# RMS norms moved into the stages that use them, and an earlier gate evacuation in the RWKV rounds, in a two-layer decoder trunk

## What is computed

```
for l in range(DEPTH):
    xn = rmsnorm(h, norm_mix_w[l])
    h = h + hybrid_mixer(xn, ...)      # RG-LRU, gated DeltaNet, RWKV-7, three sigmoid merge gates
    xn = rmsnorm(h, norm_ffn_w[l])
    h = h + peer_ffn(xn, ...)          # product-key top-k, gated experts
return rmsnorm(h, final_norm_w)

def rmsnorm(x, w):
    return x * lax.rsqrt(jnp.mean(x * x, axis=-1) + 1e-6) * w
```

## Time and profile before

| | us |
|---|---|
| median of 3 runs | 3383.24 |
| lowest, highest | 3376.41, 3383.72 |
| the profiled execution | 3370.82 |
| its span, first instruction to last | 3368.9 |
| PE busy in the span | 3245.6 |
| DVE busy | 2270.9 |
| ACT busy | 1673.8 |
| POOL busy | 161.2 |

### The profile page before, as it was taken

One profiled execution on the slowest core, in us unless ns is written; L12 is line 12 of the kernel. 1 busy time (PEld: TensorE's weight loads), 2 busy tenths in 40 slices (PEclk: granted clock), 3 DMA queues, 4 the chain that ended last, 5 costly groups with the idle time before them and its releaser, 6 DMA issues. The chain is left out here.

```text
span 3368.9 us, 73580 instructions
## 1 busy us (share of the span) xinstructions
PE 3245.6 (96%) x24714; PEld 2813.4 (84%) x24714; DVE 2270.9 (67%) x5009; ACT 1673.8 (50%) x3549; POOL 161.2 (5%) x169
## 2 busy tenths in 40 slices
PE   8999999999999999999999999999999999999998
PEld 7777778889998888888878777888898978888886
DVE  5666666655886677777666665666658866777776
ACT  5445454433296555555544443544423955555554
POOL 0101101100000000000001101011000000000000
PEclk9999999999999999999999999999999999999999
DMA  3322323223323555555432323232242245555553
GB/s 130 96 74 80 109 78 104 88 82 144 107 81 128 190 187 187 187 189 192 155 127 66 99 68 104 82 107 75 94 169 83 75 149 188 187 187 191 191 190 126
DMA packets 122237, 433.35 MB, mean 129 GB/s; under 512 B 15744, under 2 KB 18048, under 8 KB 121344
## 3 DMA queue, kind: packets, MB, share of 16 engines
q1 hardware_dynamic: 122112, 431.74, 37.4%
HBM read 430.64 MB, written 1.05 MB: 128 GB/s over the span
## 5 line engine op out<-in xcount | busy, mean ns | idle before, releaser
L2265 PE MATMUL bank<-x_both,u_parts 128*128 128x512 f32 x1536 | 557.9, 397 | 1.4 <-DVE u_parts L2385 1.4
L2249 PE MATMUL bank<-v_parts,act_high 128*128 128x512 f32 x1024 | 405.6, 396 | 4.6 <-DVE v_parts L2390 3.4
L2251 PE MATMUL bank<-v_parts,act_low 128*128 128x512 f32 x1024 | 400.0, 391 | 0.0
L2261 PE MATMUL bank<-x_both,u_parts 128*128 128x256 f32 x1536 | 399.6, 281 | 0.0
L2250 PE MATMUL bank<-v_parts,act_high 128*128 128x512 f32 x1024 | 398.9, 390 | 0.0
L298 PE MATMUL bank<-x_parts,w_parts 128*128 128x256 f32 x1248 | 394.2, 316 | 1.5 <-DVE w_parts L286 1.5
L2385 DVE TENSOR_TENSOR u_parts<-u_raw,u_parts 128x512 fp32r<-128x512 f32 x384 | 265.4, 692 | 191.6 <-ACT u_parts L2320 191.5
L299 PE MATMUL bank<-x_parts,w_parts 128*128 128x256 f32 x1248 | 352.3, 282 | 0.0
L300 PE MATMUL bank<-x_parts,w_parts 128*128 128x256 f32 x1248 | 351.4, 282 | 0.0
L2390 DVE TENSOR_TENSOR v_parts<-v_raw,v_parts 128x512 fp32r<-128x512 f32 x512 | 329.7, 685 | 28.8 <-ACT v_parts L2327 25.6
L263 PE MATMUL bank<-arena,ring 128*128 128x256 f32 x1408 | 326.3, 385 | 19.8 <-ACT zg L793 9.7
(11 more groups left out here) (353 smaller groups left out, 5650.9 us busy)
## 6 DMA issues: line engine op xcount, KB each, us to landing
v_raw<-in_v SPq DMA_DIRECT2D x256, 512.0 KB, 3.5
u_raw<-in_u SPq DMA_DIRECT2D x192, 512.0 KB, 4.1
ring<-in_w_side SPq DMA_DIRECT2D x80, 512.0 KB, 3.5
ring<-in_w_gdn SPq DMA_DIRECT2D x64, 512.0 KB, 3.5
ring<-in_w_rwkv SPq DMA_DIRECT2D x48, 512.0 KB, 5.7
ring<-in_w_gdn_side SPq DMA_DIRECT2D x32, 512.0 KB, 3.5
ring<-in_u SPq DMA_DIRECT2D x32, 512.0 KB, 3.7
u_ring<-in_u SPq DMA_DIRECT2D x32, 512.0 KB, 3.5
```

What stands on the lines that cost most here:

```text
L2249: te.matmul(ps, f32r(w_hi), f32r(x_hi), start=start, stop=False, **kw)
L2251: return te.matmul(ps, f32r(w_lo), f32r(x_hi), start=False, stop=stop, **kw)
L2261: return te.matmul(banks[r % 4][:, T:2 * T], f32r(u_lo[:, cols]), f32r(xhigh[:, k]), start=False, stop=stop)
L2265: mm = te.matmul(banks[r % 4][:, :].rearrange("p (x t) -> p x t", x=2), f32r(u_hi[:, cols]), f32r(x_both[:, :, k]), start=(k == 0), stop=( ...
```

## The change

**The norms.** `rmsnorm` becomes a class `Norm` with a method for each engine. "mixnorm" is called at the head of `rwkv_phase`'s block, "ffnnorm" at the head of `peer_topk_phase`'s; "outnorm" stays a block. With that

- the barrier between a norm and its stage is gone; every consumer waits for the tiles it needs (`ready` for tile k, `all_ready`);
- DVE multiplies tiles 0 and 1, then 2 to 4; POOL tile 5, then 6 and 7; POOL also waits for ACT's last `hw`;
- ACT takes the constant's root right behind its squares, then `hw` 0 to 4, then the root of the means, then `hw` 5 to 7;
- PE runs 15 identity matmuls where it ran 22 (none in outnorm, as before);
- mixnorm's buffers lie in `zg`, so that SP issues the parameters right behind the weight tiles.

**The rounds.** `act_side(a, i, 3)` and a root of one constant column go ahead of the wait for the variance. In the last round PE gets two more identity matmuls at level 5 and six in the state steps.

```diff
+    class Norm:
+    VEC = 5
+    def vector(self, v):
...
+        for a, b in ((0, 2), (2, self.VEC)):
+            self.scaled(v, slice(a, b)).then_inc(V.sem, V.one(f"x{a}"))
+    def tensor(self, te, idle):
...
+        turn(te, banks[1], idle)
+    def scalar(self, a):
...
+        a.activation(self.root, ones[:, 0:1], ACT.Sqrt).then_inc(S.sem, S.one())
+        weighted(range(self.VEC))
+        a.wait_ge(V.sem, V.at("ms"))
+        a.activation(rs, rs, ACT.Sqrt).then_inc(S.sem, S.one("root"))
+        weighted(range(self.VEC, KT))
+    def gpsimd(self, g):
+        g.wait_ge(self.S.sem, self.S.at(f"hw{KT - 1}"))
+        g.wait_ge(self.V.sem, self.V.at("rs"))
+        for a, b in ((self.VEC, self.VEC + 1), (self.VEC + 1, KT)):
+            self.scaled(g, slice(a, b)).then_inc(self.G.sem, self.G.one(f"x{a}"))
...
@@ rwkv_phase @@
+                rwkv_first_tiles(sp, l)
                 sp.dma_start(consts64[:, :], A["consts64"]).then_inc(pload, 16)
...
-                    elif lev and y == 0:
+                    elif lev and (y == 0 or lev == 5):
...
                     if q:
+                        if not more:
+                            turn(te, b4, 1)
                         te.wait_ge(V.sem, V.at(f"S{q - 1}", i))
...
                         side(2 * q + 7)
+                        if not more:
+                            turn(te, b4, 1)
                         te.wait_ge(V.sem, V.at(f"R{q}", i))
...
+                norm.tensor(te, 15)
                 te.wait_ge(wload, 32)
...
+                act_side(a, i, 3)
+
+                a.activation(no_root, ones[:, 0:1], ACT.Sqrt).then_inc(S.sem, S.one())
                 a.wait_ge(V.sem, V.at("var", i))
                 a.activation(va4, va4, ACT.Sqrt).then_inc(S.sem, S.one("sd"))
-                act_side(a, i, 3)
...
+                norm.vector(v)
+                norm.all_ready(v)
...
@@ peer_topk_phase @@
+                query_first_loads(sp, l)
                 clear(sp, mixer_sems)
...
+                norm.tensor(te, 15)
                 te.wait_ge(query_loaded_keys, 16)
...
+                            if t == 0:
+                                norm.ready(te, k)
```

More of the change, by code:

```diff
@@ L202, in rmsnorm, with branch_buffers @@
+    def branch_buffers():
         r = Region(BRANCH)
[L203 to L206, removed]
+        return r(KT, T), r(KT, T), r(T), r(1)
+    def rmsnorm(tag, w, dst):
+        norm = Norm(tag, w, dst, branch_buffers())
         with nc.Block() as block:
[L208 to L211, removed]
@@ L213, in _ @@
             @block.vector
             def _(v):
[L215 to L221, removed]
@@ L222, in _ @@
-                scaled(v, slice(0, VEC)).then_inc(V.sem, V.one())
-                v.wait_ge(V.sem, V.now())
+                norm.vector(v)
+                norm.all_ready(v)
             @block.tensor
             def _(te):
[L227 to L231, removed]
@@ L232, in _ @@
-                mm.then_inc(E.sem, E.one("ss"))
-                if ahead:
-                    turn(te, banks[1], 22)
+                norm.tensor(te, 0)
             @block.scalar
             def _(a):
[L238 to L242, removed]
@@ L244, in _ @@
-                a.activation(root, ones[:, 0:1], ACT.Sqrt).then_inc(S.sem, S.one())
-                a.wait_ge(V.sem, V.at("ms"))
-                a.activation(rs, rs, ACT.Sqrt).then_inc(S.sem, S.one("root"))
+                norm.scalar(a)
             @block.gpsimd
             def _(g):
-                g.wait_ge(V.sem, V.at("rs"))
-                scaled(g, slice(VEC, KT)).then_inc(G.sem, G.one())
-                g.wait_ge(G.sem, G.now())
+                norm.gpsimd(g)
     def turn(te, ps, n):
@@ L563, in rwkv_phase @@
     def rwkv_phase(l):
+        norm = Norm("mixnorm", norm_w[:, 2 * l], xn, (zg[:, 0], zg[:, 1], zg[:, 2, 0], zg[:, 2, 1, 0:1]))
         NI = KT
@@ L934, in _ @@
                 te.sem_inc(W.used, W.PRIME)
+                norm.tensor(te, 15)
                 te.wait_ge(wload, 32)
                 for s in range(2):
-                    project(te, banks[2 + s][:, 0:T], 6 + s).then_inc(E0.sem, E0.one(f"lora{s}"))
+                    for k in range(KT):
+                        if s == 0:
+                            norm.ready(te, k)
+                        mm = project(te, banks[2 + s][:, 0:T], 6 + s, ks=range(k, k + 1))
+                    mm.then_inc(E0.sem, E0.one(f"lora{s}"))
                 E.prime(te)
@@ L1025, in _ @@
             def _(a):
+                norm.scalar(a)
                 for k in range(0, KT, KT // 2):
+                    if k:
+                        norm.all_ready(a)
+                    else:
+                        norm.ready(a, 0)
+                        norm.ready(a, 2)
                     a.activation(f32r(x_parts[:, 0, k:k + KT // 2]), xn[:, k:k + KT // 2], ACT.Copy).then_inc(x_high, 1)
@@ L1921, in peer_topk_phase, with _ @@
         flat = lambda x: x.rearrange("p h k -> p (h k)")
+        norm = Norm("ffnnorm", norm_w[:, 2 * l + 1], xf[:, :], branch_buffers())
         with nc.Block() as block:
+            @block.gpsimd
+            def _(g):
+                norm.gpsimd(g)
             @block.vector
```

44 lines of the change are left out of this document (39 added, 5 removed).

## The result

| | us |
|---|---|
| before, median of 20 runs | 3377.41 (3374.43 to 3383.72) |
| after, median of 20 runs | 3388.06 (3382.21 to 3396.24) |
| ratio after / before, 95% interval | 1.0030 (1.0023 to 1.0037) |
| profiled execution of after | 3388.44, span 3386.6 |

The forecast was 3379.6 and the range 3368 to 3388: the time is outside by a hair, and its sign is the wrong one. Over the 20 runs of after the time follows the mean granted clock: 3382.21 us at 0.995, 3396.24 at 0.990.

The account below looks back on a forecast made before the run. PE, busy 3245.6 of 3368.9 us, was taken to bound the kernel. Norms -13.9, looped rounds +8.5 and last rounds +1.8 summed to -3.6 us, from 3383.24 giving 3379.6 us; range 3368 to 3388.

Parts of the forecast that it names:

- first mixnorm, means to gates: First layer's mixnorm: the gates start at 26.4 us instead of 29.99, -3.6 us.
- second mixnorm, the same: Second layer's mixnorm: by the same sum 1697.55 us instead of 1699.93, -2.4 us.
- first ffnnorm, means to the first key scores: First layer's ffnnorm: first query tile done by 803.45 us instead of 806.0, -2.55 us.
- second ffnnorm: Second layer's ffnnorm: query tiles done earlier, idle stretch and lower clock gone, -4.9 us; 1.6 lost if the clock falls.
- outnorm, means to the end: Outnorm: table load leaves the path (0.48 us), less 0.1 for POOL's second instruction, -0.4 us.
- 14 looped rounds: Looped RWKV rounds' end: table loads make the root 0.97 us late, +0.61 us a round, 8.5 us lost.
- 2 last rounds: Last RWKV rounds: L923 +0.27 us, three of eight new identity matmuls +0.65, together +0.9 each, +1.8 us.
- the clock at the round's end: Rival, ahead of L923: PE's idle stretch grows to 1.4 us, TensorE falls to 1.2 GHz, 1.6 us each; 3403 us; chance 0.08.
- The costly load: Rival, round's end: a table switch holds ACT some 1.4 us more than its row, +38 us, 3418 us; chance 0.03.

Follow-up runs that it names:

- the second trace of before: The kernel before, unchanged, executed once more for another trace; 3377.12 us.
- the kernels with late roots: The kernel before with eight, or four, roots of a constant between ACT's wait for the variance and the root; 3405.6 us with eight, 3390.42 us with four.
- the one trace: Trace of the changed kernel without the constant's root, f3 still evacuated first; median 3377.4 us, ratio 0.9999 to the kernel before.

## Why the prediction was wrong, point by point

| step | forecast | measured (profiles) |
|---|---|---|
| first mixnorm, means to gates | -3.6 | -3.7 |
| second mixnorm, the same | -2.4 | -2.5 |
| first ffnnorm, means to the first key scores | -2.55 | -2.4 |
| second ffnnorm | -4.9 | -4.7 |
| outnorm, means to the end | -0.4 | -0.9 |
| 14 looped rounds | +0.61 each | +0.57 each |
| 2 last rounds | +0.9 each | +0.3 (first layer's) |
| **sum** | **-3.6** | **-5.6** |
| falls of the clock at round ends | 0 | +9.9 |
| PE's branch, and the low clock behind it | 0 | +4.3 |
| first means later, at the start of the run | 0 | +1.2 |

The lower part is 15.4 us; with the sum it gives +9.8, the medians differ by 10.7. The two agree in part by chance, for the table is made from two single traces, and the two profiled executions differ by 17.6; the 8 us between are mostly falls at the GDN stages' edges and ends (6.7 us), a kind that the second trace of before has too. The last row isn't the change's: the first means come at 14.92 and 15.03 us in the kernels with late roots as well, whose first norm is that of before (14.13 and 13.96).

- **The mechanisms stood.** Rows 1 to 5 and 7 to 10 gave each step within 0.6 us. The second layer's query tiles kept their clock, as the sum had it (timeline after, it answers rows 5):

```profile
2489.54 0.42 DVE L216 TENSOR_SCALAR arena<-bank 128x256 f32<-128x256 f32 x1 [3.21 <-PE bank L229]
...
2494.47 3.62 PE L2133 MATMUL bank<-xf,ring 128*128 x28 [0.57 <-DVE xf L209]
...
2497.93 0.39 PE L2119 MATMUL bank<-arena 128*128 128x128 f32 x2
```

From the means to the first key scores (L2119) it is 8.39 us, where it was 13.10 before.

- **The step that failed is the clock at the round's end, a term that the sum put at nothing.** It stood as a rival only. It was named with its place, its price (1.6 us; measured 1.65) and the point from which it decides (seven rounds; six fell), and given 0.08. The argument against it was that stretches of 2.2 us stood elsewhere once with a fall and once without, and that 1.4 is well under either. That compared single stretches, while the pair at the round's end (1.36 and 0.29, with 0.44 of work between) comes fourteen times, and a place that falls once in two times at 2.2 us was no proof of safety at 1.4. In its place the runs show six falls, +9.9 us, over the whole 8.5 us that the sum had for the late roots. They also show how near the edge it lay: with 0.1 us less idle time no round of the one trace fell. What picks the rounds, seven without a fall in the first layer and six with one in the second at the same waits, stays open.
- **The branch** was in no rival. It cost +4.3 us, the second term that the sum lacked. I costed the new identity matmuls by the time they run and not by what might follow from more code on PE; why the branch is slow stays open.
- **The last rounds** were mis-sized: +0.3 instead of +0.9 with the new order, although the same matmuls cost 0.65 to 0.69 with the old one. Why they overlap the late root better I can't say.
- **The costly load** did not happen: from load to load to root the rows add up to 3.20 us with no drain. 137 table loads before, 165 after: the 28 more that were forecast.
- **The range** rested on the first three runs of before (median 3383.24). Its median over 20 was 3377.41; the same net figure from there gives 3373.8, so 6 us of the forecast's distance were hidden by a base that stood too high: it is luck that the time lies only just outside the range.

## What to carry to other kernels

When an edit lengthens a wait of TensorE inside a loop, price the clock for every turn of the loop and not by the length of the wait against others: here idle stretches of 1.36 us instead of 0.41 cost 9.9 us by the clock and 8.0 by the time they took, and ten identity matmuls in the wait saved the falls for 0.1 us a round. Don't put a function of another table set ahead of something that PE waits for; evacuate by one that needs no load (here the bias alone, 0.4 us a round saved) and apply the costly one later. And look at the branch of every outer loop on PE's queue after adding instructions, however cheap they are.

## What the runs showed of the hardware that I had not expected

- A branch on PE's queue that takes 0.47 us in one kernel takes 3.4 to 3.8 in others that have eight or nine matmuls more, in all six traces of them.
- The clock falls at the same places in repeated executions: the same six consecutive rounds in three traces (one of them with one matmul more), while the first layer's rounds, with the same waits, had none, one and one.
- TensorE stayed at 1.2 GHz for 24 us while its records show it busy for 22.69 of 23 us, in a round made of small matmuls with short waits; two of six traces have it, and none of the eight with identity matmuls in these waits.
- ACT's table load for an instruction that waits is issued ahead of the wait (in the kernel without the constant's root at 92.19, with DVE's variance from 92.42).
